# Two MLP blocks on one core: four PSUM reads a pair instead of five in the down phases, with shared accumulators folded in later

## The reference, cut to what matters

```python
def squared_relu_mlp(h, w1, w2):
    return jnp.square(jax.nn.relu(h @ w1)) @ w2      # 512 x 1024, 1024 x 4096, 4096 x 1024, float32

x = x + rms_norm(squared_relu_mlp(rms_norm(x, g[2]), mlp_w1[i], mlp_w2[i]), g[3])     # i = 0, 1
```

## Time and profile before

| what | value |
|---|---|
| median of three runs | 1768.19 us |
| the profiled execution, own time | 1768.53 us |
| its span | 1766.7 us |
| PE busy | 1726.6 us, 98% |
| DVE busy | 1079.7 us, 61% |
| ACT busy | 771.5 us, 44% |
| POOL busy | 949.3 us, 54% |

### The profile page before, as it was taken

One profiled execution on the slowest core, in us unless ns is written; L12 is line 12 of the kernel. 1 busy time (PEld: TensorE's weight loads), 2 busy tenths in 40 slices (PEclk: granted clock), 3 DMA queues, 4 the chain that ended last, 5 costly groups with the idle time before them and its releaser, 6 DMA issues.

```text
span 1766.7 us, 25913 instructions
## 1 busy us (share of the span) xinstructions
PE 1726.6 (98%) x9327; PEld 1486.1 (84%) x9327; DVE 1079.7 (61%) x1715; ACT 771.5 (44%) x1301; POOL 949.3 (54%) x583
## 2 busy tenths in 40 slices
PE   8999999999999999999999999999999999999999
PEld 6887887989898877878798989889878888888887
DVE  5458657767677779856776767777756344444200
ACT  6328645343434556554534343455357332222221
POOL 2447546554555668755555455565445544444442
PEclk9999999999999999999999999999999999999999
DMA  5532121314231313122131423232210222222232
GB/s 179 132 107 62 36 72 60 132 62 142 72 125 67 108 48 108 60 84 96 60 126 66 144 69 123 72 108 73 86 49 13 96 95 96 98 100 99 95 107 71
DMA packets 46103, 158.84 MB, mean 90 GB/s; under 512 B 5744, under 2 KB 6000, under 8 KB 46000
## 3 DMA queue, kind: packets, MB, share of 16 engines
q1 hardware_dynamic: 46000, 157.45, 26.7%
HBM read 153.10 MB, written 2.10 MB: 88 GB/s over the span
## 4 chain that ended last, share of the span: by engine, by line
PE 77%; DVE 13%; ACT 4%; issue 3%; POOL 1%; DMA 1%; SPq 0%; DVEq 0%; ACTq 0%; POOLq 0%
PE PS L2182 22%; PE PS L2183 21%; PE PS L2184 21%; DVE PS L1445 2%; DVE wl L1437 2%; PE PS L2251 2%; DVE PS L1437 2%; DVE M L1437 1%; PE PS L2287 1%; PE PS L2282 1%; DVE sqb L1437 1%; PE PS L2283 1%; DVE TL L1437 1%; DVE tmp L1437 1%; DMA raw<-weights 1%
## 5 line engine op out<-in xcount | busy, mean ns | idle before, releaser
L2183 PE MATMUL PS<-XLR,wh 128*128 128x512 f32 x1216 | 474.4, 390 | 0.0
L633 POOL TENSOR_TENSOR wl<-raw,wh 128x1024 fp32r<-128x1024 f32 x92 | 223.4, 2430 | 261.7 <-ACT wh L1416 120.8
L623 POOL TENSOR_TENSOR wl<-raw,wh 128x1024 fp32r<-128x1024 f32 x109 | 261.7, 2407 | 180.4 <-ACT wh L884 179.4
L2182 PE MATMUL PS<-XHR,wh 128*128 128x512 f32 x888 | 348.9, 393 | 6.1 <-POOL wl L772 5.8
L2184 PE MATMUL PS<-XHR,wl 128*128 128x512 f32 x888 | 346.7, 390 | 0.0
L884 ACT ACTIVATE wh<-raw 128x1024 fp32r<-128x1024 f32 x171 | 179.7, 1057 | 291.5 <-PE PS L2184 243.6
L2183 PEld LDWEIGHTS PS<-XLR,wh 128*128 128x128 f32 x1216 | 229.2, 188 | 46.9
L2182 PE MATMUL PS<-TH,wh 128*128 128x256 f32 (+1 forms) x872 | 253.1, 290 | 12.0 <-POOL TL L708 5.7
L2183 PE MATMUL PS<-TL,wh 128*128 128x256 f32 (+1 forms) x872 | 251.5, 288 | 0.0
L2184 PE MATMUL PS<-TH,wl 128*128 128x256 f32 (+1 forms) x872 | 251.3, 288 | 0.0
L2182 PEld LDWEIGHTS PS<-XHR,wh 128*128 128x128 f32 x888 | 167.6, 189 | 41.6 <-POOL wl L772 6.2
(11 more groups left out here) (370 smaller groups left out, 3406.7 us busy)
## 6 DMA issues: line engine op xcount, KB each, us to landing
raw<-weights SPq DMA_DIRECT2D x287, 512.0 KB, 3.3
X<-x_t SPq DMA_DIRECT2D x8, 256.0 KB, 8.0
out_t<-X SPq DMA_DIRECT2D x8, 256.0 KB, 4.2
KH<-rope_h SPq DMA_DIRECT2D x4, 128.0 KB, 5.0
KL<-rope_l SPq DMA_DIRECT2D x4, 128.0 KB, 5.3
QH<-XHR SPq DMA_DIRECT2D x16, 32.0 KB, 2.0
QL<-XLR SPq DMA_DIRECT2D x16, 32.0 KB, 2.0
pos_i<-positions SPq DMA_DIRECT2D x1, 256.0 KB, 8.9
```

The costliest lines, as they stand in the source:

```text
L623: pool.tensor_tensor(wl[:, WPOS[n]], raw[:, n % RING], wh[:, WPOS[n]].bitcast(F32), ALU.subtract).then_inc(w_lo, 1)
L633: pool.tensor_tensor(wl[:, s], raw[:, j], wh[:, s].bitcast(F32), ALU.subtract).then_inc(w_lo, 1)
L2182: pe.matmul(out, wa, xa, start=start, stop=False)
L2183: pe.matmul(out, wa, xb, start=False, stop=False)
```

## The change

Two banks a pair now carry two results each that were read apart. A11 and S1 share a bank; a read adds the whole bank to a new accumulator, `shared[:, u]`, in SBUF, and only in the last chunk is it added to the quarters of `M`: `fold(u)`, two DVE instructions of 128x512 whose inputs `M` and `shared` both lie in SBUF. There are four folds, at t = 1 to 4 of the last chunk, in the order pairs 3, 0, 1, 2. The last chunk itself doesn't use `shared`: its first read of a pair is two instructions into `M`. So chunks 0 to 2 read four banks a pair, each bank always in the same role (`read_bank`), and PE waits for the same read of the pair before. In chunk 0 the first three reads are plain copies. The last read of a pair moves behind the first weight sums of the next pair, `restore` with it.

In the up phases ACT rounds an odd hidden tile as soon as it is made, before it waits for the sums; DVE waits for that copy (`hid_hi`) before it makes the odd sums, and `odd_low` follows directly. In the last tile of a chunk `quad_low(S2)` goes ahead of the odd sums.

`shared` overlies two of the three buffers of the convolution's taps, so `low_taps(0)` and `low_taps(1)` move to the down phase of the last chunk of the first MLP, behind a wait for the last fold.

```diff
-READS = 5
-LAST_PRODUCT = (0, 1, 4, 5, 6)
+READS = 4
+LAST_PRODUCT = (1, 4, 5, 6)
+        shared = at("shared", A, 80 * KB, [P, QUADS, 2, HALF_S])
...
-            return (T0 + READS * u + j) % 4
+            return (T0 + j) % 4
...  ACT, hidden_odd
+                    sc.wait_ge(bank_free, T + 1)
+                    sc.activation(parts(TH, p, H21, 2), squared(1), ACT.Copy).then_inc(hid_hi, 1)
                     sc.wait_ge(sums_made, 4 * NCHUNK * layer + p + 1)
-                    sc.activation(parts(TH, p, H21, 2), squared(1), ACT.Copy).then_inc(hid_hi, 1)
...  ACT, the loop over t, and the last down phase
-                        if layer == 0 and c in (1, 2) and t == 3:
-                            sc.wait_ge(dw_low_done, 1)
-                            low_taps(c - 1)
...
+                if layer == 0:
+                    sc.wait_ge(dw_low_done, 1)
+                    sc.wait_ge(folded, 1)
+                    low_taps(0)
                 square_m(1)
                 square_m(2)
...  DVE, odd_sums
+                    v.wait_ge(hid_hi, 2 * (4 * NCHUNK * layer + p) + 2)
...  DVE, read
+                    if j == 0 and c == NCHUNK - 1:
+                        step(tt(d[:, 0:4:3], d[:, 0:4:3], first, ALU.add))
+                        out, x = d[:, 2:4], second
                     else:
+                        out = (shared[:, u], d[:, 0:2], d[:, 2:4], d[:, 1:4:2])[j]
+                        x = first if j == 3 else whole
+                    if c == 0 and j < 3:
+                        v.tensor_copy(out, x).then_inc(products_read, 1)
+                    else:
+                        tt(out, out, x, ALU.add).then_inc(products_read, 1)
+                def fold(u, done):
+                    v.wait_ge(products_read, done)
+                    d = quarters(u)
+                    for i, out in enumerate((d[:, 0:4:3], d[:, 2:4])):
+                        ins = tt(out, out, shared[:, u, i:i + 1].broadcast_to((P, 2, HALF_S)), ALU.add)
+                        if u == 2 and i == 1:
+                            sig(ins, folded, layer + 1)
+                        else:
+                            step(ins)
...  DVE, the loop over t
+                        if last and t <= 4:
+                            fold((t + 2) % 4, READS * QUAD0[n0])
                         if last and t == 1:
                             restore(KT // 2 - 1, READS * QUAD0[n0])
...  PE, open_bank
+                    if u:
+                        pe.wait_ge(products_read, READS * (QUAD0[n0] + u - 1) + j + 1)
                     else:
+                        pe.wait_ge(bank_free, T0 - 3 + j)
```

More of the change, by code:

```diff
@@ L375, in build @@
         products_made, products_read = sem("products_made"), sem("products_read")
-        restored = sem("restored")
+        restored, folded = sem("restored"), sem("folded")
         last_m_hi, last_m_lo = sem("last_m_hi"), sem("last_m_lo")
@@ L503, in build, with read_bank @@
         SUM_A, SUM_B = PS[:, STAT], PS[:, RB]
-        def read_bank(T0, u, j):
-            return (T0 + READS * u + j) % 4
+        def read_bank(T0, j):
+            return (T0 + j) % 4
         def parts(buf, p, i, n=1):
@@ L1221, in mlp @@
                     quad_high(n0, h)
+                if layer == 0:
+                    low_taps(1)
                 n = n0 + 2 * quads
@@ L1784, in odd_sums @@
                 def odd_sums(c, t):
+                    p = 4 * c + t // 2
+                    v.wait_ge(hid_hi, 2 * (4 * NCHUNK * layer + p) + 2)
                     t1, t3, t4, t2 = [t_sums[:, i * HALF_S:(i + 1) * HALF_S] for i in range(4)]
@@ L1804, in read @@
                     v.wait_ge(products_read, r)
[L1805 to L1813, removed]
-                    else:
-                        ins = tt(out, out, x, ALU.add)
-                    ins.then_inc(products_read, 1)
+                    d, bank = quarters(u), PS[:, read_bank(T0, j)]
+                    whole = in_halves(bank)
+                    first, second = [whole[:, i:i + 1].broadcast_to((P, 2, HALF_S)) for i in range(2)]
+                    if layer == c == u == j == 0:
+                        v.wait_ge(dw_low_done, 1)
+                    if j == 0 and c == NCHUNK - 1:
+                        step(tt(d[:, 0:4:3], d[:, 0:4:3], first, ALU.add))
+                        out, x = d[:, 2:4], second
+                    else:
+                        out = (shared[:, u], d[:, 0:2], d[:, 2:4], d[:, 1:4:2])[j]
[13 more added lines that the diff above has]
+                            step(ins)
                 def restore(u, done):
@@ L1838, in mlp @@
                         else:
-                            odd_sums(c, t)
-                            if last:
-                                odd_low(c, t)
                             if t == CHUNK - 1:
                                 quad_low(n0, 0, S2)
+                            odd_sums(c, t)
+                            odd_low(c, t)
+                            if t == CHUNK - 1:
                                 quad_sum(n0, 0, S3)
-                            if not last:
-                                odd_low(c, t)
                         if t == 4:
@@ L1864, in mlp @@
                         quad_low(n0, u, S3)
-                        read(c, u, 0)
+                        if u:
+                            read(c, u - 1, 3)
+                            if last:
+                                restore(u - 1, READS * (QUAD0[n0] + u))
                         if more:
                             quad_sum(n0, u + 1, S2)
-                        read(c, u, 1)
-                        if last and u:
-                            restore(u - 1, READS * (QUAD0[n0] + u))
+                        read(c, u, 0)
                         if more:
@@ L1874, in mlp @@
                             quad_low(n0, u + 1, S2)
-                        read(c, u, 2)
-                        if more:
                             quad_sum(n0, u + 1, S3)
-                        read(c, u, 3)
+                        read(c, u, 1)
                         if more:
                             quad_low(n0, u + 1, S4)
-                        read(c, u, 4)
+                        read(c, u, 2)
+                    read(c, quads - 1, 3)
                     if last:
@@ L2536, in open_bank @@
                     n0, T0, _ = down_block(layer, c)
-                    g = READS * u + j
-                    if g < 4:
-                        pe.wait_ge(bank_free, T0 - 3 + g)
-                    else:
-                        pe.wait_ge(products_read, READS * QUAD0[n0] + g - 3)
-                    return PS[:, read_bank(T0, u, j)]
+                    if u:
+                        pe.wait_ge(products_read, READS * (QUAD0[n0] + u - 1) + j + 1)
+                    else:
+                        pe.wait_ge(bank_free, T0 - 3 + j)
+                    return in_halves(PS[:, read_bank(T0, j)])
                 def down_quads(c):
-                    first, second = slice(0, HALF_S), slice(HALF_S, S)
                     for u in range(down_block(layer, c)[2]):
[L2548 to L2555, removed]
+                        x = open_bank(c, u, 0)
+                        product(c, u, A11, x[:, 0], H11)
+                        product(c, u, S1, x[:, 1], H_T1)
+                        y = open_bank(c, u, 1)
+                        product(c, u, A12, y[:, 0], H21)
+                        z = open_bank(c, u, 2)
+                        product(c, u, S2, z[:, 1], H_T2)
+                        product(c, u, S4, y[:, 1], H22)
+                        product(c, u, A22, z[:, 0], H_T4)
+                        product(c, u, S3, open_bank(c, u, 3)[:, 0], H_T3)
                 def after_quads(c, t):
```

4 lines of the change are left out of this document (2 added, 2 removed).

## The result

The changed kernel takes 1772.01 us (median of 20 runs, 1769.09 to 1776.56), beside 1767.09 us for the kernel before (20 runs, 1762.0 to 1770.42). The ratio is 1.0034, with a 95% interval of 1.0026 to 1.0042: slower by 6.0 us (4.6 to 7.4), where +8.3 was forecast. The ratio is taken over all the runs; the two medians are 4.9 us apart, and the two profiled executions, of which the after one took 1771.59 us, only 3.06.

A forecast was written before the change was run, and what follows sets the result against it. PE, busy 98% of the span, was taken as the bound. 2 x (6.2 folds + 1.7 clock) - 7.5 reads = +8.3 us gave a 1776.5 us median; own range 1771.9 to 1779.5, 8-in-10 range 1764 to 1781.5.

The forecast's parts named there:

- The sign, the place and the cause: Slower by 8.3 us; PE waits 5 to 7 us for DVE's `TL` at each down tile, because folds make DVE late.
- new reads (taps moved): Both MLPs' bank reads: PE's waits for `M` and POOL go, 5.9 us idle plus 0.16 us restart each, 7.5 us gained.
- taps: First MLP's last down phase: 16 copies of 0.39 us go to ACT; taken as nothing, at most 3.1 us.
- early rounding: Up phases: PE's 2.8 us wait for POOL in chunk 0 moves by -0.5 to +0.5 us; taken as nothing.
- folds and clock: Last chunk's up phase and down tile: 6.2 us of lateness plus 1.7 us of clock loss, in each of two MLPs.
- the margin of 1.9 us: Chunk 1, pair 1: read 1 of pair 0 ends about 404.1, A12 is due at 405.98, so PE's wait goes.
- the 0.7 us wait for ACT: Up phases: DVE waits the same 0.7 us before the odd sums; `odd_low` ends unchanged, the sums 0.7 us later.
- a bank wait of 0.36 us: Behind POOL's wait in chunk 0: no longer waited for at that product, paying for sums 0.4 us late.
- 6.2 us late at t = 6: Last chunk's up phase: folds blocked by POOL add 9.6 to 10.7 us, minus 4.05 us slack; 5.6 to 6.7 late.
- the 1.1 us that hang on it: Fold at t = 3: if it begins before POOL it costs 2.5 us, each MLP 1.1 us less, 2.1 in all.
- Clock: After each down tile's stall of some 6 us: one half-speed stretch, 1.7 us lost per MLP, bounds 0 and 2.7.

## Why the prediction was right, and where it was not

The sign, the place and the cause were right: a gain of some 8 us at the banks is outweighed by the folds, which come out as PE's wait for DVE's `TL` at the down tile. By its steps:

| step | predicted, us | measured, us |
|---|---|---|
| new reads (taps moved) | -7.5 | -8.8 (-11.3 to -6.4), alone |
| taps | 0 (at most 3.1) | not run alone |
| early rounding | 0 (POOL's wait ±0.5) | +5.7 (3.7 to 7.8) in the kernel before; +0.7, +2.5, +4.0 (each about ±3) on the new reads |
| folds and clock | +15.8 | +15.4 (11.8 to 18.9) alone in before; +10.8 (about ±3) inside the change |
| sum | +8.3 | +6.0 (4.6 to 7.4) |

*Reads.* Right, but for chunk 0. Four of the five waits for `M` and `wl` in each MLP went; at chunk 0's pair 1, PE still waits 0.52 us in each (0.36 and 0.65 before), so the margin of 1.9 us did not hold there. In the changed kernel with the old order of rounding this wait is absent, so it seems to belong to that step. (It is absent without fold instructions too, but there PE had run at 0.50 just ahead of it.)

*Taps.* Nothing in the traces waits for them, and the kernel with the new reads alone, in which they are moved, lost nothing that can be seen. They now start at 578.4 us, where the earlier trace rows has 370.3.

*Early rounding.* This step failed. What it says of the 0.7 us wait for ACT and of POOL's wait came out: POOL's wait grew by 0.3 us. But it also held that a bank wait of 0.36 us would pay for the sums' 0.4, and in the kernel before, alone, that bank wait grew to 1.31 us instead. It left out the weight sum that the new order moves behind `odd_low` at the last tile of chunks 0 to 2, a move that the section on the change doesn't name either. There the sum starts with POOL's pair and takes 1.80 us instead of 0.70, which makes DVE late for the lead tile. So the blocking that the prediction priced for the folds was at work in a second place, and there it was priced at nothing. No run moves this sum alone. On the new reads most of the waits that it lengthens are gone, so less of it shows: 4.0 us by the runs without folds, 2.5 beside DVE's folds, 0.7 beside POOL's. Which of these three is right stays open.

*Folds.* Right in mechanism and close in size. DVE was forecast 6.2 us late at t = 6 and is 6.5 us late; the pairs were to cost 2.7, 2.5, 2.5 to 3.6 and 1.4 us, and took 3.52, 2.47, 3.53 and 1.41, with the restore at 0.69 instead of 1.61. At t = 3 POOL's row begins first, by 0.01 us, and the pair took the dearer time (twice the 1.1 us that hang on it is 2.2, not 2.1). The lateness became PE time: 5.43 us of waiting, and about 1 us by which the three matmuls between the two waits were slow at 0.50.

*Clock.* About right in sum, but not as reasoned. The fall came where it was put, and lasts longer: 10.2 us with 7.0 us of work in each, a loss of 3.5 us by half of the busy time, where 1.7 was forecast. But it did not come on top of all the others. In the two traces the four falls of before at 310.6, 604.2, 884.1 and 1269.8, each 3.4 us long and nearly all busy, so 6.8 us of loss in all, are absent after: the net would be 0.2 us. That pair of traces is not typical, as every run's mean granted clock shows. Since the clock is either 1.00 or 0.50, twice the difference of the mean from 1, times the span, is an estimate of the time at half speed:

| kernel | runs | mean granted clock | at half speed, us |
|---|---|---|---|
| before, beside the experiments | 13, 35 and 16 | 0.9915, 0.9914, 0.9910 | 30 to 32 |
| changed | 20 | 0.9876 | 44 |
| new reads alone | 6 | 0.9915 | 30 |
| no fold instructions | 8 | 0.9895 | 37 |
| early rounding in before | 11 | 0.9898 | 36 |
| folds in before | 6 | 0.9858 | 50 |

The profiled executions have 0.990 and 0.988, 35 and 42 us, so they are 7 apart where the runs are 12 to 14 apart; that goes with their times, 3.06 us apart where the runs are 6.0. The two falls at the down tiles make 20.5 us. So on the average some 7 us of other falls are missing, not 13.6, and the net loss is 7.0 less about 3.5: an estimate of 3.5 us, where 3.4 were added. That this fits is partly luck, since each fall cost twice what was forecast and others went missing, which nothing had foreseen. It also bears on the other prices. The kernel without fold instructions has 7 us more at half speed than the new reads alone, up to 3.5 us of the 4.0 that rounding costs there. Early rounding in the kernel before has 3.9 us of longer waits in the two MLPs and 4 us more at half speed, up to 2 us of loss, which together about make its 5.7. One of its stretches, in chunk 0:

```profile
309.18:312.59 3.41, 3.41 (x18) 3.41 (x17) 2.78 (x6) 1.89 (x4) 3.21 (x3) 0.50 0.12 23
```

The folds add 18 us or more at half speed alone and 7 inside the change, which could make most of the difference between 15.4 and 10.8. Why a fall comes in one kernel and not in another is left open.

The errors partly cancelled. Taken one after the other, the steps are -8.8 for the reads, +4.0 for rounding and +10.8 for the folds with the clock, against -7.5, 0 and +15.8: 1.3 us more gain, 4.0 more cost, 5.0 less cost. The total of +8.3 is 2.3 us above the measured one, and that it is so near owes something to the last two. Alone in the kernel before, rounding and folds cost +5.7 and +15.4, so the prices of the parts do not simply add.

## What to carry to other kernels

A row of the same kind elsewhere in the trace (here one restore, 0.68 us alone and 1.61 behind POOL) prices an added instruction; then lay it tile by tile against what the other engine does at that moment, since work that follows the same tile coincides again and again. When an order is changed, do this for every instruction that changes its place, not only for the wait that the change is about. An instruction with two SBUF inputs that must go somewhere may be cheaper on the slower engine, in a stretch where that engine waits anyway: eight folds of 1.3 us on POOL left PE no wait at the down tile, while on DVE, at 0.69 us bare and 1.4 on the average, they cost PE 5.4 us in each MLP. And before two traces are compared by their falls of the clock, compare the mean granted clock of all the runs.

## What the runs showed of the hardware

A DVE instruction of two columns with both inputs in SBUF took as long beside POOL as POOL's own of 512 columns (2.54 us for two, against 0.35 with POOL idle). Cutting such instructions to two columns saves their own length, about 1 us a pair, and not the wait for POOL; moving one input to PSUM saves the wait (four pairs in 5.6 us instead of 10.9, and 1.8 instead of 5.4 us of wait at the down tile). It holds for a weight sum from two SBUF inputs into PSUM too: 0.70 us ahead of POOL's pair, 1.80 when it starts with it. The blocking goes both ways: POOL's 2.40 us low part took 2.85 us with a fold beside it. And the same wait of PE can be followed by a fall of the clock or not: behind 3.1 us of standing in chunk 0 the granted clock fell to 0.50 without folds and stayed at 1.00 in the changed kernel; why it did not fall there isn't settled.
